# Weaving the attention of one token block into output projection and MLP of the block before

## The chip, the cores and the metric

The kernel runs on one NeuronCore of one Trainium2 chip. The metric is device microseconds (us) from the start to the end of one execution; the median of several executions is compared. The core has five engines that run at the same time and meet only at semaphores: PE (TensorE, the matmuls), DVE (VectorE), ACT (ScalarE), POOL (GpSimd), and SP (SyncE), which issues the DMAs here. Each engine takes its instructions strictly in the order in which they were written for it: a wait holds up everything behind it.

## The reference

One layer over 2048 prompt tokens (16 tiles of 128) and 64 sample tokens (tile 17, against 512 cached keys). All matrices are float32; each big product is computed as three fast products of a high part and a rest (hi·hi, hi·lo, lo·hi).

```python
gla_in, (sq, sk, sv), gate = project(xp, *lw)       # RMSNorm, x @ w_in (1024 x 3088)
S_p, o_g = gla_prompt(*gla_in)                      # gated linear attention, 4 heads
o_s = sb_prompt(sq, sk, sv)                         # stick-breaking attention, 8 heads of 64
xp = finish(xp, o_g, gate, o_s, *tail)

def sb_block(q, q_pos, k, v, k_pos):                # causal, 128 queries at a time
    z = einsum(q, k) * SB_HD ** -0.5
    log_beta = log_sigmoid(z)
    l = where(mask, log_sigmoid(-z), 0.0)
    c = cumsum(l, axis=3, reverse=True) - l         # from the last key to the first
    w = where(mask, exp(log_beta + c), 0.0)
    return einsum(w, v)

def finish(x, o_gla, gate, o_sb, gla_norm_g, w_out, norm2_g, w_up, w_down):
    mix = concatenate([og, o_sb])
    h = x + mix @ w_out                             # 1024 x 1024
    u = rmsnorm(h, norm2_g) @ w_up                  # 1024 x 4096
    return h + square(relu(u)) @ w_down             # 4096 x 1024
```

The causal mask makes attention grow with the position: tile t of the prompt has t + 1 tiles of 128 keys, the sample tile has 5.

## The kernel before

Five phases run one after the other, each with its own semaphores and an all-engine barrier at its end: `phase_project`, `phase_gla`, `phase_attention` (line 1043), `phase_output`, `phase_mlp`. They hand data on through DRAM.

`phase_attention` goes over heads outside and over 25 units inside; a unit is one query tile with up to 8 (or, cut in two, up to 8 at a time of 16) key tiles. There are 200 units with 1128 tiles of 128 x 128 scores, 141 for each head. A unit passes through these steps: PE makes the logits `z` (lines 1156 and 1157, and 1159 for the mask); ACT takes |z| (1213), exp (1224) and ln (1229); DVE makes the negated softplus (1251), sets the scan's start value (1257 or 1261) and runs the reverse scan over the keys (1267), and for a cut unit saves the sum (1272); ACT makes the weights (1219); PE transposes them tile by tile (1169); DVE copies them to SBUF (1281); PE multiplies them with the values (1185, in two instructions for each tile); DVE copies the result out (1290). `slot` on each engine fixes by hand which step of which unit comes next. `z` is double buffered, so that the logits of unit u + 1 wait for the scan of unit u - 1. The operands of a head are loaded one head ahead (`load_head`), those of head 0 during `phase_gla`.

`phase_output` has all 17 tiles in a pipeline: transpose `mix` (1396), split it, 48 matmuls of 512 columns with `w_out`, which was split during attention by POOL (1406), add x (1462), norm (1440, 1478, 1480, 1464), transpose (1414), split, store h and its transposed halves to DRAM.

`phase_mlp` has 4 token blocks (4, 4, 4 and 5 tiles, the last with 576 columns in two cuts of 288). For each block it goes over 16 generations of 256 hidden columns: `up` (1616), relu and square, `down` (1630), and DVE adds each result into `ya` (1752). Each generation's weights are loaded, ACT makes the high part, POOL the rest of `w_up` (1710) and DVE the rest of `w_down` (1733); the halves are double buffered. The matmuls of a generation read:

```python
for c in range(KC):
    for bank, at, size in cuts:
        mm = pe.matmul(pu[:, f, bank, 0:size], w[:, p, c, f * P:(f + 1) * P], xx[:, b % 2, c, at:at + size],
                       start=(i == 0 and c == 0), stop=(i == 2 and c == KC - 1))
```

Of the kernel before, what the change touches and what calls it, by code (L numbers as in the profile page):

```python
# [7 lines left out]

# [11 lines left out]
P = 128  # L20
# [626 lines left out]
def phase_gla(nc, gqk, gv, sgate, la, gla_g, state_in, ident, sum_mats, end_mat, score_mask, mix, new_state, pad_values, load_first):  # L647


    with Pool(nc, "gl") as m:  # L650
# [41 lines left out]
        s_am, s_vz, s_hin, s_hv = m.sem("am"), m.sem("vz"), m.sem("hin"), m.sem("hv")  # L692
# [23 lines left out]
        def _(sp):  # L716
# [15 lines left out]
            def slot(h, p, stages, sample):  # L732
# [11 lines left out]
                if 3 in stages:  # L744
                    h2, p2, t2 = before(h, p, 2)
                    sp.wait_ge(s_mo, t2 + 1)
                    sp.dma_start(mix[bass.ds(t2 * P, P), 0:512], mo[:, p2]).then_inc(s_md[p2], 16)
# [7 lines left out]
                if isinstance(h, int) and h * 2 + p == 1:  # L755
                    sp.wait_ge(s_vz, 1)
                    load_first(sp, s_hin, s_hv)

            pipeline(sp, slot)
            sp.wait_ge(s_hin, 80)  # L760
            sp.wait_ge(s_hv, 48)
# [116 lines left out]
        def _(dve):  # L878
            dve.memset(pad_values, 0.0).then_inc(s_vz, 1)
# [122 lines left out]
def attention_operands(m):  # L1002

    kt = m.sb("kt", [P, 2, KEYS], F32R)
    qh = m.sb("qh", [P, 2, ROWS], F32R)
    ql = m.sb("ql", [P, 2, ROWS], F32R)
    v = m.sb("v", [P, 2, KEYS // P, HD])
    return kt, qh, ql, v


def load_head(sp, operands, h, p, qT, kT, new_v, cache_v, s_in, s_v):

    kt, qh, ql, v = operands

    def head(ap):
        return ap[bass.ds(h, 1)].rearrange("o p k -> p (o k)")

    sp.dma_start(raw(kt[:, p]), head(kT)).then_inc(s_in, 16)
    for half in range(2):
        ps = slice(64 * half, 64 * half + 64)  # L1020
        sp.dma_start(raw(qh[ps, p]), head(qT)[0:64]).then_inc(s_in, 16)
        sp.dma_start(raw(ql[ps, p]), head(qT)[64:128]).then_inc(s_in, 16)
    cols = bass.ds(h * HD, HD)
    sp.dma_start(v[:, p, 0:SEQ // P], new_v[0:SEQ, cols].rearrange("(t p) c -> p t c", p=P)).then_inc(s_v, 16)
    sp.dma_start(v[:, p, SEQ // P:NEW_KEY_COL // P], cache_v[:, cols].rearrange("(t p) c -> p t c", p=P)).then_inc(s_v, 16)
    sp.dma_start(v[0:DEC, p, NEW_KEY_COL // P], new_v[SEQ:SEQ + DEC, cols]).then_inc(s_v, 16)
# [16 lines left out]
def phase_attention(nc, operands, qT, kT, new_v, cache_v, ident, diag_mask, mix, w_out, wh, wl):  # L1043
# [13 lines left out]
    with Pool(nc, "sb") as m:  # L1057
# [186 lines left out]
        def _(dve):  # L1244
# [58 lines left out]

            turns(dve, slot)

# [534 lines left out]
```

## Time and profile before

| | us |
|---|---|
| median of 3 runs | 3550.8 |
| lowest, highest | 3543.4, 3557.4 |
| profiled execution, span | 3553.5 |
| of it projection and GLA (to 1012) | 1012 |
| attention (1012 to 1804) | 792 |
| output projection (1804 to 2066) | 262 |
| MLP (2066 to the end) | 1487 |

The profile is that of one execution; its page shows nothing around the span, and its span lies 2.7 us above the median and inside the range of the runs. Busy times are sums of durations of instructions. For PE they overlap and their ends are modelled, so PE's true pace is read from counts of matmuls in a stretch in which it never waits, not from the mean duration. A wait is put down to the engine that released it last.

### The profile page before, as it was taken

What the parts mean: (1) busy time and instruction counts of PE and PEld (TensorE: products, weight loads), DVE (VectorE), ACT (ScalarE), POOL (GpSimd) and SP (SyncE); (2) the same over time, 40 slices, a digit from 0 to 9 for tenths busy, and PEclk for the clock granted to TensorE, in tenths of its full rate; (3) what the DMA queues carried; (4) which work ended last, traced back from release to release, by engine and by line L of the source; (5) the groups of instructions that cost most, each with busy time, mean ns of one, the idle gap of its engine ahead of it and who ended that gap; (6) DMA issues with size and microseconds to landing.
All of it is one profiled execution on the core that took longest, in us unless ns stands there. A gap on an engine that the chain in (4) does not pass through costs nothing. (4 is left out here: it accounts for less than half of the span.)

```text
span 3553.5 us, 48415 instructions
## 1 busy us (share of the span) xinstructions
PE 3228.6 (91%) x17416; PEld 2740.7 (77%) x17416; DVE 2017.8 (57%) x2853; ACT 1362.9 (38%) x1711; POOL 581.0 (16%) x379
## 2 busy tenths in 40 slices
PE   6999999979977787877779969999999999999999
PEld 5878777867767676777768758888888888899898
DVE  3545453459979899999933334444444444444444
ACT  3332423112248787788822222222222222222221
POOL 2131313013340000000000022222222222211210
PEclk8999999978869899899989989999999999999999
DMA  4535353342242211122035673335323523242221
GB/s 156 185 132 184 119 177 115 107 128 80 80 114 55 56 37 44 32 55 55 7 108 189 189 258 101 96 95 190 102 97 95 195 94 94 95 143 76 83 83 39
DMA packets 283612, 385.83 MB, mean 109 GB/s; under 512 B 50049, under 2 KB 195730, under 8 KB 280402
## 3 DMA queue, kind: packets, MB, share of 16 engines
q1 hardware_dynamic: 283474, 384.03, 34.6%
q8 instruction: 81, 1.33, 0.2%
q14 instruction: 57, 0.47, 0.0%
HBM read 295.26 MB, written 88.74 MB: 108 GB/s over the span
## 5 line engine op out<-in xcount | busy, mean ns | idle before, releaser
L1710 POOL TENSOR_TENSOR ml_ul<-ml_ur,ml_uh 128x2048 fp32r<-128x2048 f32 x63 | 293.4, 4657 | 1136.0 <-ACT ml_uh L1658 1136.0
L1752 DVE TENSOR_TENSOR ml_ya<-ml_ya,ml_pd 128x1024 f32<-128x1024 f32 x272 | 331.6, 1220 | 259.2 <-PE ml_pd L1630 259.2
L1740 DVE TENSOR_TENSOR ml_r<-ml_r 128x512 f32<-128x512 f32 (+1 forms) x128 | 84.9, 705 | 495.6 <-ACT ml_th L1688 495.6
L1267 DVE TENSOR_TENSOR_SCAN sb_g<-sb_z,sb_g,sb_a 128x639 f32<-128x639 f32 (+7 forms) x200 | 342.4, 1712 | 4.9
L1630 PE MATMUL ml_pd<-ml_dh,ml_th 128*128 128x512 f32 x1088 | 336.4, 390 | 1.6 <-DVE ml_ya L1752 1.6
L1630 PE MATMUL ml_pd<-ml_dl,ml_th 128*128 128x512 f32 x1088 | 335.5, 390 | 0.0
L1630 PE MATMUL ml_pd<-ml_dh,ml_tl 128*128 128x512 f32 x1088 | 335.1, 389 | 0.0
L1156 PE MATMUL sb_z<-hd_kt,hd_qh 128*128 128x512 f32 (+3 forms) x360 | 157.0, 436 | 163.1 <-DVE sb_g L1267 87.4
L1665 ACT ACTIVATE ml_dh<-ml_dr 128x2048 fp32r<-128x2048 f32 x64 | 122.8, 1919 | 473.8 <-PE ml_pd L1630 469.8
L1185 PE MATMUL sb_po<-hd_v,sb_wt 128*128 128x64 f32 x2256 | 303.8, 287 | 0.0
L1185 PEld LDWEIGHTS sb_po<-hd_v,sb_wt 128*128 128x128 f32 x2256 | 293.4, 206 | 3.5
L1682 ACT ACTIVATE ml_r<-ml_pu 128x512 f32<-128x512 f32 (+1 forms) x128 | 78.2, 611 | 536.4 <-PE ml_pu L1616 536.4
L1616 PE MATMUL ml_pu<-ml_xh,ml_uh 128*128 128x512 f32 (+1 forms) x1280 | 264.8, 353 | 21.0 <-DMA ml_xh<-h_t_hi 20.4
L1616 PE MATMUL ml_pu<-ml_xl,ml_uh 128*128 128x512 f32 (+1 forms) x1280 | 264.9, 353 | 1.6 <-DMA ml_xl<-h_t_lo 1.6
L1616 PE MATMUL ml_pu<-ml_xh,ml_ul 128*128 128x512 f32 (+1 forms) x1280 | 263.3, 352 | 0.0
L1616 PEld LDWEIGHTS ml_pu<-ml_xh,ml_uh 128*128 128x128 f32 x1280 | 215.8, 189 | 53.2 <-DMA ml_xh<-h_t_hi 20.8
L1616 PEld LDWEIGHTS ml_pu<-ml_xl,ml_uh 128*128 128x128 f32 x1280 | 215.2, 189 | 32.5 <-DMA ml_xl<-h_t_lo 2.4
L1616 PEld LDWEIGHTS ml_pu<-ml_xh,ml_ul 128*128 128x128 f32 x1280 | 214.5, 188 | 30.1
L1630 PEld LDWEIGHTS ml_pd<-ml_dh,ml_tl 128*128 128x128 f32 x1088 | 204.3, 188 | 43.0
L1630 PEld LDWEIGHTS ml_pd<-ml_dl,ml_th 128*128 128x128 f32 x1088 | 204.2, 188 | 42.8
L1630 PEld LDWEIGHTS ml_pd<-ml_dh,ml_th 128*128 128x128 f32 x1088 | 201.9, 188 | 45.5 <-DVE ml_ya L1752 5.8
L1156 PEld LDWEIGHTS sb_z<-hd_kt,hd_qh 128*128 128x128 f32 x360 | 75.0, 208 | 209.6 <-DVE sb_g L1267 110.7
(168 smaller groups left out, 5702.6 us busy)
## 6 DMA issues: line engine op xcount, KB each, us to landing
ml_ur<-in_w_up SPq DMA_DIRECT2D x64, 1024.0 KB
ml_dr<-in_w_down SPq DMA_DIRECT2D x64, 1024.0 KB, 4.9
pj_wr<-in_w_in SPq DMA_DIRECT2D x48, 1024.0 KB, 5.5
k_t<-pj_stT SPq DMA_DIRECT2D x21, 512.0 KB, 3.2
hd_kt<-k_t SPq DMA_DIRECT2D x8, 1344.0 KB, 9.3
pj_xb<-in_x SPq DMA_DIRECT2D x17, 512.0 KB, 6.6
q_t<-pj_stT SPq DMA_DIRECT2D x17, 512.0 KB, 3.2
hd_qh<-q_t SPq DMA_DIRECT2D x16, 544.0 KB, 12.3
```

Of the source, the lines that this page charges most:

```text
L1156: pe.matmul(dst, qh[:, p, t * P:(t + 1) * P], keys, start=True, stop=False)
L1185: mm = pe.matmul(po[:, tt % 2, 0:HD], wt[:, place(gi, 4, NGR), c * P:(c + 1) * P], v[:, p, key], start=(first and j == 0 and c == 0), stop ...
L1267: ins = dve.tensor_tensor_scan(g[:, u % 2, n - 2::-1], z[:, u % 2, n - 1:0:-1], a[:, place(u, 3), n - 2::-1], g[:, u % 2, n - 1:n], ALU.ad ...
L1616: mm = pe.matmul(pu[:, f, bank, 0:size], w[:, p, c, f * P:(f + 1) * P], xx[:, b % 2, c, at:at + size], start=(i == 0 and c == 0), stop=(i ...
L1630: mm = pe.matmul(pd[:, q, n * 512:(n + 1) * 512], tt[:, p, f, j * P:(j + 1) * P], w[:, p, f, n * 512:(n + 1) * 512], start=(i == 0 and f = ...
L1665: act.activation(dh[:, p], dr[:], ACT.Copy).then_inc(s_dh, 1)
L1682: act.activation(dst, src, ACT.Relu).then_inc(s_r, 1)
L1710: pool.tensor_tensor(ul[:, p], ur[:], raw(uh[:, p]), ALU.subtract).then_inc(s_ul, 1)
L1740: dve.tensor_tensor(r[:, f, 0:n], r[:, f, 0:n], r[:, f, 0:n], ALU.mult).then_inc(s_sq, 1)
L1752: dve.tensor_tensor(ya[:, j], ya[:, j], pd[:, q], ALU.add).then_inc(s_ya, 1)
```

## The change

`phase_attention`, `phase_output` and `phase_mlp` become one `phase_stream`. The loop over heads moves inside a loop over the four token blocks. The attention of block 0 runs alone; that of block b + 1 is spread evenly over the output projection and MLP of block b; under block 3 there is none. Where each engine does what is worked out when the program is built: `dense_order` gives the order of PE's dense work, `Plan` gives each piece a time from fixed costs of a matmul, and `weave` puts the three parts of each attention slot at even distances into it, on each engine in the same way. Nothing of this phase is in a hardware loop.

```diff
+def dense_order():
+    for j in range(BT):
+        yield "mix", 0, 0, j
+    for b in range(NB):
+        nt = NTS[b]
+        for g in range(OG):
+            for j in range(nt):
+                yield "out", b, g, j
+                if g == OG - 1 and j >= 2:
+                    yield "hid", b, 0, j - 2
+        for j in range(nt - 2, nt):
+            yield "hid", b, 0, j
+        yield "up", b, 0, 0
+        for g in range(NFG):
+            if g + 1 < NFG:
+                yield "up", b, g + 1, 0
+            for j in range(nt):
+                yield "down", b, g, j
+            if b + 1 < NB and g >= NFG - 2:
...
+                    yield "mix", b + 1, 0, j
+def weave(plan, ranges, streams, parts):
+    for b in range(NB):
+        lo, hi = plan.region[b]
+        first, n = ranges[b]
+        slots = n + 5
+        for i in range(slots):
+            s = i - 1
+            def unit(k):
+                return first + s - k if 0 <= s - k < n else None
+            for k, part in enumerate(parts):
+                part(unit)
+                streams.to(lo + (hi - lo) * (i + (k + 1) / len(parts)) / slots - 1.0)
+    streams.to(plan.total + 1e9)
```

What PE's slot holds, for unit s of the block (`u(k)` is unit s - k):

```diff
+            def part0(u):
+                if u(2) is not None:
+                    transposes(u(2))
+
+            def part1(u):
+                if u(-1) is not None:
+                    logits(u(-1))
+
+            def part2(u):
+                if u(3) is not None:
+                    values(u(3))
```

ACT's three parts are exp and ln of unit s, the weights of unit s - 1, and |z| of unit s + 1. DVE's are the copy of the transposed weights of unit s - 2, the softplus and start value of unit s, and the scan of unit s with the copy of the result of unit s - 3. SP loads the next job's operands where a job's first unit comes by. The dense work of each engine lies between the parts.

A unit now has at most 4 key tiles (`UT = 4`, 512 columns), which makes 336 units: 32, 64, 96 and 144 in the four blocks, with 80, 208, 336 and 504 score tiles. Keys, queries and values are loaded for each head and block (40 instead of 21 key tiles for each head), one job ahead. `a` has two buffers instead of three, `tp` one bank instead of two:

```diff
-        a = m.sb("a", [P, 3, 1024])
+        a = m.sb("a", [P, 2, 512])
-        wt = m.sb("wt", [P, 4, 512])
+        wt = m.sb("wt", [P, 3, 512])
-        z = m.ps("z", [P, 2, 1024])
-        tp = m.ps("tp", [P, 2, 512])
+        z = m.ps("z", [P, 2, 512])
+        tp = m.ps("tp", [P, 512])
+        dp = m.ps("dp", [P, BANKS, 512])
```

All dense results go through the four banks of `dp` in turn. A bank is free again when ACT (relu) or DVE (all else) has read it:

```diff
+            def free(k):
+                if k >= BANKS:
+                    if plan.by_act[k - BANKS] - (plan.by_act[k - BANKS - 1] if k > BANKS else 0):
+                        pe.wait_ge(s_fa, plan.by_act[k - BANKS])
+                    else:
+                        pe.wait_ge(s_fd, plan.by_dve[k - BANKS])
```

The output projection works in 256 columns, in four generations of `w_out` for each block, which take turns in the buffers of `w_up` and `w_down` and are loaded and split anew for each block (72 generations of each buffer instead of 64). The weight halves are single buffered, and POOL makes the rests of both:

```diff
+                        mm = pe.matmul(dp[:, k % BANKS, 0:FG], xx[:, c, j * P:(j + 1) * P], ww[:, c, :],
+                                       start=(q == 0 and c == 0), stop=(q == 2 and c == KC - 1))
...
+            def up_splits():
+                for i in range(NB * GENS):
+                    yield gen_start(plan.u_end, i)
+                    act.wait_ge(s_ur, 16 * (i + 1))
+                    if i:
+                        act.wait_ge(s_full, plan.u_end[i - 1])
+                        act.wait_ge(s_ul, 2 * i)
+                    for k in range(2):
+                        c = slice(4 * k, 4 * k + 4)
+                        act.activation(uh[:, c], ur[:, c], ACT.Copy).then_inc(s_uh, 1)
...
+            def down_rests():
...
+                        pool.tensor_tensor(dl[:, k], dr[:, k], raw(dh[:, k]), ALU.subtract).then_inc(s_dl, 1)
```

h is built and kept in `ya` in SBUF: x is loaded there, the projection is added, then each MLP result; its norm and transposed halves go straight into `xh` and `xl`. DVE adds `down` results in pieces of 512 columns (544 instead of 272 of 1024). The attention result goes to SBUF (`ms`), only the GLA half of `mix` through DRAM. `phase_gla` no longer loads head 0.

## Rows read from the trace of the kernel before

**Rows 1.** The page's head.
```profile
span 3553.5 us, 48415 instructions
```

**Rows 2.** Busy by stage: us, busy (instructions) of PE, PEld, DVE, ACT, POOL, PEclk, DMA.
```profile
1012.50:1804.20 791.70, 620.84 (x4240) 558.82 (x4240) 715.85 (x1160) 625.63 (x803) 26.99 (x16) 0.91 0.22 51
1804.20:2066.00 261.80, 226.82 (x1088) 185.51 (x1088) 82.00 (x70) 55.95 (x71) 12.68 (x35) 0.93 0.57 180
2066.00:3553.50 1487.50, 1473.47 (x7104) 1250.62 (x7104) 648.35 (x593) 384.88 (x384) 293.40 (x63) 0.99 0.34 113
```

**Rows 3.** Who waited for whom after 1015: us in total, times, longest.
```profile
PE sb_z L1156 <- DVE sb_g L1267: 87.4, 95, 1.7
PE ml_pu L1616 <- DMA ml_xh<-h_t_hi: 20.4, 1, 20.4
```

**Rows 4.** Stretches of the MLP: all engines; the last block's; its L1630 alone.
```profile
2500.00:3000.00 500.00, 499.03 (x2202) 413.06 (x2201) 221.88 (x207) 137.27 (x138) 104.39 (x24) 1.00 0.35 114
...
3150.00:3450.00 300.00, 300.00 (x1755) 270.54 (x1754) 127.24 (x117) 71.58 (x70) 57.66 (x12) 1.00 0.26 82
...
3150.00:3450.00 300.00, 161.16 (x699) 129.29 (x698) 1.00 0.26 82
```

**Rows 5.** PE in attention, in order of time: start, us, instruction.
```profile
1386.38 0.50 PE L1156 MATMUL sb_z<-hd_kt,hd_qh 128*128 128x512 f32 x1 [1.50 <-DVE sb_ssum L1272]
...
1387.47 1.72 PE L1185 MATMUL sb_po<-hd_v,sb_wt 128*128 128x64 f32 x14
...
1388.92 0.92 PEld L1169 LDWEIGHTS sb_tp<-sb_idt,sb_w 128*128 128x128 f32 x8
```

**Rows 6.** Start of attention, and what its first four units take: start, us, instruction.
```profile
1015.42 0.34 SPq L1106 DMA_DIRECT2D sb_idt<-in_ident  x1
...
1020.74 0.48 DVE L1267 TENSOR_TENSOR_SCAN sb_g<-sb_z,sb_g,sb_a 128x127 f32<-128x127 f32 x1
...
1030.83 1.55 DVE L1267 TENSOR_TENSOR_SCAN sb_g<-sb_z,sb_g,sb_a 128x639 f32<-128x639 f32 x1
```

**Rows 7.** DVE in attention by shape: busy us, mean ns, idle before.
```profile
L1281 DVE COPY sb_wt<-sb_tp 128x512 f32<-128x512 f32 x208 | 141.1, 679 | 20.2 <-PE sb_tp L1169 19.9
...
L1267 DVE TENSOR_TENSOR_SCAN sb_g<-sb_z,sb_g,sb_a 128x511 f32<-128x511 f32 x16 | 20.4, 1275 | 1.0
...
L1251 DVE SCALAR_TENSOR_TENSOR sb_a<-sb_z,sb_a 128x512 f32<-128x512 f32 x16 | 10.9, 682 | 0.4
...
L1261 DVE TENSOR_TENSOR sb_g<-sb_ssum,sb_a 128x1 f32<-128x1 f32 x64 | 10.2, 159 | 6.2 <-issue 0.4
```

**Rows 8.** One ACT step of a unit of 512 columns.
```profile
1215.09 0.63 ACT L1224 ACTIVATE sb_a<-sb_a 128x512 f32<-128x512 f32 x1
```

**Rows 9.** The last tile's way through the output projection's norm.
```profile
2043.65 1.21 DVE L1462 TENSOR_TENSOR ot_hb<-ot_pp,ot_xb 128x1024 f32<-128x1024 f32 x1
...
2048.44 1.97 PE L1414 MATMUL ot_tb<-ot_idt,ot_hn 128*128 128x128 f32 x8 [7.02 <-DVE ot_hn L1464]
...
2051.50 1.22 DVE L1456 TENSOR_TENSOR ot_sl<-ot_tb,ot_sh 128x1024 fp32r<-128x1024 f32 x1 [3.12 <-ACT ot_sh L1434]
```

**Rows 10.** Lines of the MLP: ns least/median/most, first and last start.
```profile
L1710 POOL TENSOR_TENSOR ml_ul<-ml_ur,ml_uh x63: 4609/4615/4826, 2081.2 to 3471.6; 128x2048 fp32r<-128x2048 f32 x63
...
L1740 DVE TENSOR_TENSOR ml_r<-ml_r x128: 676/691/759, 2088.6 to 3522.9; 128x512 f32<-128x512 f32 x96, 128x576 f32<-128x576 f32 x32
```

**Rows 11.** A DMA of a head's operands: KB, us from issue to landing.
```profile
hd_ql<-q_t SPq DMA_DIRECT2D x16, 544.0 KB, 14.3
```

**Rows 12.** Attention with short units and with long ones; one instruction of the first.
```profile
1200.00:1250.00 50.00, 40.52 (x245) 37.54 (x244) 38.91 (x69) 32.43 (x50) 0.00 (x0) 0.76 0.45 99
1650.00:1700.00 50.00, 38.69 (x287) 34.92 (x287) 49.28 (x75) 41.98 (x49) 0.00 (x0) 0.98 0.00 1
...
1223.24 0.22 DVE L1290 COPY sb_os<-sb_po 128x64 f32<-128x64 f32 x1 [3.46 <-issue]
```

**Rows 13.** DVE's last instruction of the kernel.
```profile
3548.25 1.22 DVE L1752 TENSOR_TENSOR ml_ya<-ml_ya,ml_pd 128x1024 f32<-128x1024 f32 x1 [1.50 <-PE ml_pd L1630]
```

More of the change, by code:

```diff
@@ new lines, with attention_jobs @@
+NTS = [BT] * FULL_BLOCKS + [LAST_BT]
+TOKENS = [BT * P] * FULL_BLOCKS + [BT * P + DEC]
+W = LAST_BT * P
+FG = 256
+FC = FG // P
+NFG = D_FF // FG
+OG = D // FG
+GENS = OG // 2 + NFG
+BANKS = 4
+UT = 4
+NK = BT * FULL_BLOCKS + BT
+Job = namedtuple("Job", "block heads keys sample")
+Unit = namedtuple("Unit", "job e h tile n lo first last")
+def attention_jobs():
+    jobs = []
+    for b in range(NB):
+        jobs += [Job(b, (h,), BT * (b + 1), False) for h in range(SB_HEADS)]
+    jobs += [Job(NB - 1, (h, h + 1), PAST // P + 1, True) for h in range(0, SB_HEADS, 2)]
+    return jobs
@@ new lines, in attention_units @@
+def attention_units(jobs):
+    units = []
+    for k, job in enumerate(jobs):
+        for e, h in enumerate(job.heads):
+            for i in range(1 if job.sample else BT):
+                n = job.keys if job.sample else BT * job.block + i + 1
+                hi = n
+                while hi > 0:
+                    lo = (hi - 1) // UT * UT
+                    units.append(Unit(k, e, h, BT if job.sample else i, hi - lo, lo, hi == n, lo == 0))
+                    hi = lo
+    return units
@@ L1091, in turns @@
-        def turns(eng, slot):
-            def unit(s, last):
-                return lambda k: s - k if 0 <= s - k and not (last and s - k >= NU) else None
-            for s in range(LEAD):
-                slot(0, s, unit(s, False))
-            with eng.Fori(0, SB_HEADS // 2 - 1) as i:
-                for s in range(LEAD, NU + LEAD):
-                    slot(i, s, unit(s, False))
-            for s in range(LEAD, NU + LEAD):
-                slot(SB_HEADS // 2 - 1, s, unit(s, True))
+        gb = m.sb("gb", [P, D])
@@ new lines, in transposes, with values @@
+            def transposes(u):
+                pe.wait_ge(s_w, u + 1)
+                if u >= 1:
+                    pe.wait_ge(s_wt, u)
+                for c in range(units[u].n):
+                    mm = pe.transpose(tp[:, c * P:(c + 1) * P], w[:, u % 2, c * P:(c + 1) * P], idt[:])
+                mm.then_inc(s_tr, 1)
+            def values(u):
+                un = units[u]
+                p = un.job % 2
+                tt = tiles_done[u]
+                if u == job_first[un.job]:
+                    pe.wait_ge(s_v[p], v_need[un.job])
+                if un.first and tt >= 1:
+                    pe.wait_ge(s_of, tt)
+                pe.wait_ge(s_wt, u + 1)
+                for c in range(un.n):
+                    mm = pe.matmul(po[:, tt % 2 * HD:(tt % 2 + 1) * HD], wt[:, u % 3, c * P:(c + 1) * P],
+                                   v[:, p, un.e * jobs[un.job].keys + un.lo + c],
+                                   start=(un.first and c == 0), stop=(un.last and c == un.n - 1))
+                mm.then_inc(s_pv, 1)
```

1163 lines of the change are left out of this document (542 added, 621 removed).

## The prediction

> **What bounds the kernel now.** I read the table by stage first, then each stage for the wait that ends last. Attention and what follows take 3553.5 - 1012.5 = 2541 us of the span [rows 1, 2]; the 1012 us before are untouched. Two different engines bound this part. In the MLP PE is busy 1473 of 1487 us at clock 0.99, and in 500 us of it PE issues 2202 matmuls of 512 columns, one in 0.227 us [rows 2, 4]: that is PE's pace, and nothing of it can be hidden. The output projection is bound by PE too (227 of 262 us). In attention DVE is busy 716 of 792 us while PE's busy time is 621 us at clock 0.91 [rows 2], and PE's largest wait there is that of the logits for DVE's scan [rows 3]. So for 792 us PE waits on DVE, and for 1487 us DVE is busy only 648. The change lays the two over each other. The question is what PE's work adds up to, and how much of it the in-order queues let through.
>
> **PE's sum after the change.** Paces first, at full clock. 512 columns: 0.227 us. 288 columns: in the last block's stretch 699 of 1755 matmuls are of 512 columns and take 159 us; the other 1056 share 141 us, 0.134 each [rows 4]. The trace has no run of split products of 256 columns; on the line through the two paces they take 0.121. The bounds are 0.114 (half of a 512) and 0.134 (a 288); I take the line. A score tile of attention costs: logits 1.09 us for 8 tiles, 0.136; values 14 instructions in 1.72 us, less some 0.2 for the last one's drain, two for each tile, 0.22 to 0.23; transpose 8 in 0.92, 0.115 [rows 5]. With the mask that is 0.50.
>
> - MLP: 5568 matmuls of 512 and 1536 of 288 columns: 1264 + 206 = 1470 us. Unchanged; the trace's own stage agrees once its start is taken off.
> - Output projection: 17 tiles x 4 x 24 = 1632 matmuls of 256 columns, 198 us (before 816 of 512, 185 us): +13 us (bounds +1 to +34).
> - Its 272 transposes: 272 x 0.129 (the slower of the paces of a transpose, since fewer stand together) = 35 us.
> - Attention of blocks 1 to 3: 1048 tiles x 0.50 = 524 us. The 80 tiles of block 0 are in the lead-in.
>
> Lead-in. Attention starts at 1015.4 and its first scan is at 1020.7, on operands loaded during GLA [rows 6]. Now the constants and five loads of job 0 are issued first (about 0.4 us for each issue), and land some 4 to 8 us later (14.3 us was for a head of 544 KB beside others [rows 11]; the pieces are now 128 to 256 KB): first scan at about 1027, +6 us (bounds +2 to +14). Then 32 units of 1 to 4 tiles: the first four of before go from scan to the scan of the fifth in 10.1 us, of which the fifth's longer softplus is 0.4: 2.4 us a unit [rows 6], 77 us. The last unit needs three more slots, then the first tiles are transposed and split: dense work begins at about 1111.
>
> Removed and put at nothing more: the barriers and DMA waits between phases, 20.4 us at the MLP's start [rows 3] and PE's idle time in the projection's stage (262 us, 227 busy [rows 2]), the round trips of h through DRAM and the loop turns. They are gaps in the table of stages and aren't in the new sum.
>
> Floor: 1111 + 1470 + 198 + 35 + 524 = 3338.
>
> Added on PE's path. **The norm** stands four times between the last projection tile and `up`. The last tile of before shows the chain: add at 2043.65, square, POOL, scale, transposes at 2048.44, rest done at 2052.7, 9.1 us with PE idle for 7.0 before its transposes [rows 9]. It is now in smaller pieces, but POOL may be in a half split of 4.6 / 2 = 2.3 us [rows 10] when the norm's step reaches it: 8 us each, 32 us. In blocks 0 to 2 attention matmuls lie nearby, but PE's queue is in order and they don't move past the waiting transposes. **Tail:** DVE's last add to the end of the store, 5 us as before [rows 1, 13]. That gives 3375, the least that the new order allows. **Turn of the block:** y must leave `ya` before x comes in, two transfers of 512 KB behind each other, under 10.9 us of projection work for each column group: mostly hidden, 5 us in all (bounds 0 to 30).
>
> **What the queues cost.** Attention 1 to 3 is spread over about 390 us of dense PE time each. With attention's own matmuls a slot of PE is (390 + 104) / 69 = 7.2 us, (390 + 168) / 101 = 5.5 us and (390 + 252) / 149 = 4.3 us. Now DVE, for a full unit: copy 0.68, softplus 0.68, start value 0.16, scan 1.28, sum 0.16 (as the start value) [rows 7], with the steps between them about 3.05 us. Block 3's 144 units (112 full) need 342 + 61 = 403 us of DVE; the dense work beside them 16 x (4 steps on the hidden columns of 0.69 [rows 10] and 8 adds of 512 columns, a little over half of the 1.22 of 1024 columns [rows 9], 0.65) = 127, and 23 for projection and norm. That is 553 of 641 us, 86%. Smaller units are no gain here: 200 units become 336, and 64 pairs of `ssum` steps become 200, +43 us of DVE; moved off DVE are the 64 splits of `w_down`. ACT has about 2.6 us for a full unit (four steps of 0.63 [rows 8]), 470 us in this stretch, 73%. POOL has 288 halves of 2.3 us, 665 us in all, hidden in 2440.
>
> But shares don't decide; the round trip does. Logits of unit u + 1 wait for the scan of unit u - 1, so two slots can't be shorter than: logits 0.7, |z| 0.6, exp and ln 1.26, softplus and start 0.95, scan and sum 1.5, six hand-overs of about 0.1: 5.6 us [rows 5, 7, 8], plus what dense work stands in ACT's and DVE's queues between these steps, on average another 2 to 2.7 us (a split half of 1024 columns, 1.0; a relu, 0.6; an add, 0.65). About 8.0 us against two slots of 14.4, 11.0 and 8.6. In block 1 this never ends last, in block 2 where splits meet (15 us), in block 3 often: four split halves in each of some 14 generations, each of which can put 1.0 us into the trip, are 56 us. Beside `down` DVE has 3.05 + 1.9 adds of 0.65 = 4.3 us a slot and its waits for the step in front, against PE's 4 x 0.50 + 2.6 = 4.6; I put 0.3 us on each of some 80 such slots, 24 us. Together 80 + 15 + 5 = 100 us. This is the weakest term: bounds 0 (all slack is enough) and 300 (below). I take 100 since the trip lies just under the slot in one block of three.
>
> **Sum:** 3375 + 5 + 100 = 3480 for this execution; the median of the runs is 2.7 us below its span, so 3477, 2.1% below 3550.8. Its own range is 3430 to 3530.
>
> **The rivals.**
> - **PE alone sets the time.** The queues' slack suffices and PE never waits in blocks 1 to 3: 3375 to 3430, say 3380. For it: PE's waits for the scan in attention were 0.9 us on average and 1.7 at most [rows 3], and there are 3 us of slack in a slot of block 1. Against it: 86% of DVE in block 3.
> - **The round trip sets the time (slower).** If dense work in ACT's and DVE's queues makes the trip 12 us for two slots rather than 8, block 3 takes 149 x 6.0 = 894 us instead of 641, and block 2 606 instead of 558: 3380 + 253 + 48 = 3681. The place is the wait of `logits` for the scan. It decides from a trip of about 10.8 us (5.4 us a slot): 149 x (5.4 - 4.3) = 164 us eats the whole gain. For it: `z`, `tp` and `a` lost buffers and every piece of dense work sits inside the trip. Against it: 2.4 us a unit was reached for short units [rows 6].
> - **The clock.** Beside short units the granted clock was 0.76, with PE as busy (40.5 of 50 us) as in a stretch at 0.98 (38.7 us); in the first, all engines stood still for some 3 us at the loop's turn [rows 12]. The levels are 1.2 and 2.4 GHz, so 0.91 over attention [rows 2] is full clock with stretches at half. If the woven 1676 us ran at 0.91, they cost 166 us more: 3380 + 166 = 3546, no change. Against it: the MLP's dense matmuls at 0.99 to 1.00 [rows 4] are between the attention's now. By the Trainium skill (TensorE: Matmul & The Clock Gate, "Why this matters for your kernels") an idle PE goes to the low clock and sustained matmuls bring it back; by that rule, only the four norms and the lead-in would run slow.
> - **POOL and DVE block each other.** The rests of `w_down` move to POOL, which is then busy for 27% of the phase. If a step of DVE on the hidden columns (both inputs in SBUF, 256 of them) had to wait for a running POOL half, that is 256 x 0.27 x 1.15 = 80 us of DVE, of which the 64 in block 3's stretch count, 20 us, and some in block 2's: 3505. Against it: such steps took 676 to 759 ns with POOL busy beside them [rows 10], so nothing waits within its duration. The Trainium skill (SBUF — State Buffer, "Who interferes with whom") states it as a lock that makes the second instruction wait in full; it speaks against moving work to POOL.
> - **Loads come late.** If a job's operands took the 14.3 us of [rows 11] in the lead-in, 8 jobs last 14.3 instead of 9.6 us: +38, 3520.
>
> **Chances.** Forecast 0.42; PE alone 0.20; round trip 0.18; clock 0.09; POOL 0.05; loads 0.06. A difference under 0.5% (18 us) can't be told from none in this kernel. Faster by more (below 3533): the forecast, PE alone, POOL and most of the loads, 0.72. Within: the clock's case and bits of its neighbours, 0.09. Slower: the round trip and a bit, 0.19. The range that should hold the time 8 times in 10 is 3380 to 3640: it leaves out half of "PE alone" and about half of "round trip".
>
> **What will show it.** The first scan near 1027 and the first projection matmul near 1111 (right within 15 us). Stretches in block 1's part with PE without waits and at clock 1.0. In block 3's part (about 1900 to 2600) waits of PE's logits for the scan of 50 to 100 us in all; over 200 is the round trip, under 20 is PE alone. Four gaps of about 7 us before the norm's transposes. The last block at the old pace, 480 to 490 us. DVE's durations for the hidden steps above 0.8 us, or its waits beside POOL, would show the lock. Wrong altogether it would be if PE's pace for 256 columns, or for attention's short matmuls between dense ones, is not what [rows 4, 5] give: each 10 ns on the 1632 matmuls and on attention's some 4400 instructions in blocks 1 to 3 are 16 and 44 us.

## The result, and the profile after

| | before | changed |
|---|---|---|
| median, us | 3554.1 (4 runs) | 3710.4 (4 runs) |
| lowest, highest | 3543.4, 3560.3 | 3701.3, 3711.5 |
| profiled execution, span | 3553.5 [rows 1] | 3699.6 |
| attention, projection and MLP, from 1015 on | 2538 | 2685 |

The ratio is 1.0428, with a 95% interval of 1.0407 to 1.0449: the changed kernel is 4.3% slower. The forecast was 3477 and its range ended at 3640: it was 233 us too low and wrong in sign. The woven order itself is not what costs: the experiments end with the same weave at 3456 us, after one change to what DVE reads, one to which buffer a weight generation uses and one to a small place of the order.

Busy time by stage of the changed kernel. The columns are those of [rows 2], with the DMA's GB/s behind. The stages are the dense work of blocks 0, 1, 2 and 3 (the lead-in before them took 102 us), the first three with the attention of the next block in them, the last with none.

```profile
1117.00:1692.00 575.00, 528.51 (x2779) 443.58 (x2777) 346.09 (x555) 254.21 (x424) 178.18 (x79) 0.96 0.30 90
1692.00:2343.00 651.00, 593.12 (x3223) 502.00 (x3224) 442.11 (x714) 330.99 (x551) 182.24 (x81) 0.96 0.29 89
2343.00:3126.00 783.00, 683.82 (x3818) 578.91 (x3817) 558.94 (x938) 428.68 (x727) 185.26 (x82) 0.94 0.27 82
3126.00:3695.00 569.00, 516.49 (x3019) 464.17 (x3018) 206.72 (x261) 123.17 (x186) 173.72 (x78) 0.94 0.20 65
```

No engine is busy all the time: PE is at 87 to 92% in the four dense stages and DVE never above 71%. By the forecast's paces blocks 0 to 2 need 411 us of PE each without attention (1536 matmuls of 512 columns, 384 of 256, 64 transposes, 8 us for the norm), with 208, 336 and 504 tiles at 0.50 then 515, 579 and 663, and block 3 needs 499. They took 60, 72, 120 and 70 more. The last block is the telling one: it has no attention at all, yet it lost as much as the first two. So the loss can't be only attention's round trip. Who PE waited for from 1015 on, the lead-in included (us in all, times, longest):

```profile
PE st_z L1366 <- DVE st_g L1649: 68.3, 43, 5.2
PE st_dp L1487 <- DVE st_ya L1730: 43.9, 24, 2.3
PE st_z L1366 <- DVE st_ssum L1654: 42.0, 22, 4.8
PE st_dp L1466 <- POOL st_ul L1758: 25.6, 4, 6.4
...
PE st_tp L1377 <- DVE st_wt L1662: 20.2, 13, 3.2
...
PE st_dp L1414 <- DMA st_mg<-mix: 12.8, 3, 12.4
PE st_dp L1487 <- DVE st_xl L1684: 12.7, 3, 4.2
...
PE st_dp L1487 <- issue: 6.0, 1, 6.0
```

DVE is behind most of these, in the logits (L1366), in `down` (L1487) and in the transposes (L1377), though it is idle for 29% of the third stage and for more of the others. A wait of 5.2 us for one scan is four scans long. So I looked at how long DVE's own instructions lasted (ns least/median/most, first and last start; then the groups by shape: busy us, mean ns, idle before):

```profile
L1718 DVE TENSOR_TENSOR st_tl<-st_r,st_th x128: 691/760/2811, 1197.1 to 3662.0; 128x512 fp32r<-128x512 f32 x96, 128x576 fp32r<-128x576 f32 x32
L1642 DVE TENSOR_TENSOR st_g<-st_ssum,st_a x200: 159/159/2376, 1130.4 to 3071.9; 128x1 f32<-128x1 f32 x100
...
L1718 DVE TENSOR_TENSOR st_tl<-st_r,st_th 128x512 fp32r<-128x512 f32 x96 | 165.4, 1723 | 3.3
L1642 DVE TENSOR_TENSOR st_g<-st_ssum,st_a 128x1 f32<-128x1 f32 x200 | 81.9, 409 | 18.2
L1716 DVE TENSOR_TENSOR st_r<-st_r 128x512 f32<-128x512 f32 x96 | 76.2, 794 | 261.2 <-ACT st_th L1606 261.2
```

L1718 (hidden rest, `tl = r - th`) takes 1.72 us on average. In the kernel before, the same step (L1743) took 677 to 753 ns. L1642 (start value of the scan, one element in each partition) takes 0.41 us against 0.159 [rows 7], and 2.38 at most. One L1718 in two is held up: 63 of the 128 took 2.71 to 2.81 us, the others at most 0.76. Over all instructions that is about 131 us more on L1718 (128 x 1.02), 50 on L1642 and 11 on L1716 (the square): 192 us of DVE. All three take both operands from SBUF. L1649, the scan, reads `a` from SBUF and `z` from PSUM and keeps its 1277 ns.

One place of the last block, in order of time (start, us, instruction; in brackets the idle time before it and what ended it):

```profile
3416.23 5.25 POOL L1758 TENSOR_TENSOR st_ul<-st_ur,st_uh 128x1024 fp32r<-128x1024 f32 x2 [8.05 <-ACT st_uh L1555]
...
3418.45 0.81 DVE L1716 TENSOR_TENSOR st_r<-st_r 128x576 f32<-128x576 f32 x1 [6.92 <-ACT st_th L1606]
...
3419.29 2.81 DVE L1718 TENSOR_TENSOR st_tl<-st_r,st_th 128x576 fp32r<-128x576 f32 x1
...
3422.02 2.47 DVE L1730 TENSOR_TENSOR st_ya<-st_ya,st_dp 128x512 f32<-128x512 f32 x4
...
3422.75 1.10 PE L1487 MATMUL st_dp<-st_dh,st_th 128*128 128x512 f32 x2 [2.28 <-DVE st_ya L1730]
...
3423.65 1.05 PE L1487 MATMUL st_dp<-st_dl,st_th 128*128 128x512 f32 x2
```

POOL's two halves run from 3416.23 to 3421.48. L1718 is released at 3419.29, inside the second half, and ends at 3422.10, 0.62 us behind POOL: it did its work when POOL had finished. Behind it DVE's queue holds the adds that free the banks of `dp`, so PE waits 2.28 us. It then goes on at half pace: 0.425 us a matmul instead of 0.227 until about 3426.2, 8 matmuls in 3.46 us where full clock needs 1.82. So this collision costs PE 2.3 us of waiting and 1.6 of slow clock. In attention the same happens to the smallest instruction of all:

```profile
2811.27 4.75 POOL L1765 TENSOR_TENSOR st_dl<-st_dr,st_dh 128x1024 fp32r<-128x1024 f32 x2 [19.41 <-ACT st_dh L1565]
2811.31 2.38 DVE L1642 TENSOR_TENSOR st_g<-st_ssum,st_a 128x1 f32<-128x1 f32 x1
...
2815.12 0.50 PE L1366 MATMUL st_z<-st_kt,st_qh 128*128 128x512 f32 x1 [0.42 <-DVE st_g L1649]
```

It comes 0.04 us behind POOL's start and ends as POOL's first half does (2.37 us, half of the 4.75). These rows fit the rule in the Trainium skill (SBUF — State Buffer, "Who interferes with whom"): a DVE instruction with two SBUF inputs and a GpSimd instruction that reads SBUF use one read port, and the second is blocked in full. That such a lock costs the time is theory A. Theory B is that the in-order queues and the round trip cost it, and that the long durations lie in DVE's slack.

### The profile page after: what moved, and what is told of

The parts are those of the page before. It is cut to its first block and busy times, and to the rows that moved or that the text cites. A ratio compares the mean times of both kernels' runs of the same rounds, so it can differ in the third digit from the quotient of the medians.

```text
span 3699.6 us, 49868 instructions
## 1 busy us (share of the span) xinstructions
PE 3302.8 (89%) x18184; PEld 2798.4 (76%) x18184; DVE 2193.4 (59%) x3664; ACT 1498.3 (40%) x2479; POOL 975.7 (26%) x588
## 5 line engine op out<-in xcount | busy, mean ns | idle before, releaser
L1758 POOL TENSOR_TENSOR st_ul<-st_ur,st_uh 128x1024 fp32r<-128x1024 f32 x144 | 370.1, 2591 | 961.9 <-ACT st_uh L1555 961.9
L1765 POOL TENSOR_TENSOR st_dl<-st_dr,st_dh 128x1024 fp32r<-128x1024 f32 x144 | 342.8, 2402 | 939.5 <-ACT st_dh L1565 939.5
L1730 DVE TENSOR_TENSOR st_ya<-st_ya,st_dp 128x512 f32<-128x512 f32 x544 | 365.5, 682 | 167.1 <-PE st_dp L1487 164.8
L1487 PE MATMUL st_dp<-st_dh,st_th 128*128 128x512 f32 x1088 | 381.4, 423 | 62.5 <-DVE st_ya L1730 43.9
L1716 DVE TENSOR_TENSOR st_r<-st_r 128x512 f32<-128x512 f32 (+1 forms) x128 | 101.2, 790 | 486.7 <-ACT st_th L1606 486.7
L1649 DVE TENSOR_TENSOR_SCAN st_g<-st_z,st_g,st_a 128x127 f32<-128x127 f32 (+3 forms) x336 | 371.5, 1106 | 19.7 <-DVE st_g L1642 0.5
L1487 PE MATMUL st_dp<-st_dh,st_tl 128*128 128x512 f32 x1088 | 377.4, 420 | 0.0
L1487 PE MATMUL st_dp<-st_dl,st_th 128*128 128x512 f32 x1088 | 372.7, 419 | 0.0
L1390 PEld LDWEIGHTS st_po<-st_v,st_wt 128*128 128x128 f32 x2256 | 322.2, 204 | 28.8 <-DVE st_ms L1672 2.0
L1466 PE MATMUL st_dp<-st_xh,st_uh 128*128 128x512 f32 (+1 forms) x1280 | 307.8, 373 | 30.7 <-POOL st_ul L1758 25.6
L1390 PE MATMUL st_po<-st_v,st_wt 128*128 128x64 f32 x2256 | 310.6, 280 | 2.1 <-DVE st_ms L1672 1.6
L1487 PEld LDWEIGHTS st_dp<-st_dh,st_th 128*128 128x128 f32 x1088 | 212.2, 201 | 114.0 <-DVE st_ya L1730 54.0
L1366 PE MATMUL st_z<-st_kt,st_qh 128*128 128x128 f32 (+3 forms) x336 | 137.7, 410 | 131.5 <-DVE st_g L1649 68.3
L1487 PEld LDWEIGHTS st_dp<-st_dl,st_th 128*128 128x128 f32 x1088 | 213.4, 200 | 42.3
L1487 PEld LDWEIGHTS st_dp<-st_dh,st_tl 128*128 128x128 f32 x1088 | 213.3, 201 | 42.0
```

The lines of the kernel that those rows point to most:

```text
L1366: pe.matmul(dst, qh[:, p, q0:q0 + P], keys, start=True, stop=False)
L1390: mm = pe.matmul(po[:, tt % 2 * HD:(tt % 2 + 1) * HD], wt[:, u % 3, c * P:(c + 1) * P], v[:, p, un.e * jobs[un.job].keys + un.lo + c], sta ...
L1466: mm = pe.matmul(dp[:, k % BANKS, 0:size], ww[:, c, f * P:(f + 1) * P], xx[:, c, at:at + size], start=(q == 0 and c == 0), stop=(q == 2 an ...
L1487: mm = pe.matmul(dp[:, k % BANKS, :], tt[:, p, f, j * P:(j + 1) * P], ww[:, f, n * 512:(n + 1) * 512], start=(q == 0 and f == 0), stop=(q ...
L1649: ins = dve.tensor_tensor_scan(g[:, u % 2, n - 2::-1], z[:, u % 2, n - 1:0:-1], a[:, u % 2, n - 2::-1], g[:, u % 2, n - 1:n], ALU.add, ALU ...
L1730: dve.tensor_tensor(part, part, dp[:, k % BANKS], ALU.add).then_inc(s_fd, 1)
```

## The experiments

**POOL only writes.** The rests become constants, so part of the weight products is left out; POOL's steps keep their length and their place.

```diff
-pool.tensor_tensor(ul[:, c], ur[:, c], raw(uh[:, c]), ALU.subtract).then_inc(s_ul, 1)
+pool.wait_ge(s_ul, 2 * i + k)
+pool.memset(raw(ul[:]), 0.0).then_inc(s_wo, 1)
+pool.wait_ge(s_wo, wo())
+pool.memset(raw(ul[:, 4 * k:4 * k + 2]), 0.0).then_inc(s_ul, 1)
```

> The changed kernel, with POOL's rests of the weights replaced by memsets of about the same length (128x2048, then 128x512 elements, for each half). They write the rests as zero, so the low parts of the weights are left out of the result; POOL reads no SBUF. Everything else, the order and the waits included, is as in the changed kernel. Theory A (POOL's reading subtractions block DVE's steps with two SBUF inputs: in the changed kernel the step on line 1718 took 1722 ns on average and that on line 1642 409 ns, where 700 and 159 are its cost alone): both fall to their cost alone, some 190 us of DVE time go, and with PE's slow stretches behind them the kernel comes down from 3700 to between 3460 and 3540. Theory B (the round trip from logits to the scan through the queues sets the time): the trip keeps its steps, so the time stays at 3660 or more.

3517.3 us (one run). Its DVE, grouped by shape, has no long instruction left, while POOL is as busy as before (1.81 us and a second memset of 0.53 for each half):

```profile
L1719 DVE TENSOR_TENSOR st_tl<-st_r,st_th 128x512 fp32r<-128x512 f32 x96 | 66.5, 692 | 3.3
L1643 DVE TENSOR_TENSOR st_g<-st_ssum,st_a 128x1 f32<-128x1 f32 x200 | 31.9, 160 | 18.2
...
L1766 POOL MEMSET st_ul<- 128x2048 f32 x144 | 260.7, 1811 | 951.7 <-ACT st_uh L1556 943.2
```

63 of the 128 L1719 lie beside a memset, as 63 of L1718 lay beside a rest, and keep their time. So it is POOL's reading that matters, not its length or the order of the queues: some 190 us.

**DVE reads one SBUF input.** Everything is computed. The square is made in place in the PSUM bank, the rest is taken from there, and the start value gets its subtrahend as a scalar operand.

```diff
-dve.tensor_tensor(top, ssum[:], a[:, u % 2, n - 1:n], ALU.subtract)
+dve.tensor_scalar(top, a[:, u % 2, n - 1:n], ssum[:], -1.0, ALU.subtract, ALU.mult)
...
-dve.tensor_tensor(r[:, f, 0:n], r[:, f, 0:n], r[:, f, 0:n], ALU.mult).then_inc(s_rr, 1)
+    dve.tensor_tensor(dp[:, k % BANKS, 0:size], dp[:, k % BANKS, 0:size], r[:, f, at:at + size], ALU.mult).then_inc(s_rr, 1)
...
+    ins = dve.tensor_tensor(tl[:, gg % 2, f, at:at + size], dp[:, k % BANKS, 0:size], raw(th[:, gg % 2, f, at:at + size]), ALU.subtract)
```

> The changed kernel with full arithmetic and POOL's work untouched; only DVE's steps get one SBUF input. The square of the hidden values is made in the PSUM bank (bank times the relu in SBUF), the rest is bank minus high part, so each of the two reads PSUM and SBUF; the banks of up are then freed by DVE. The start value of the scan is made by a tensor_scalar with the sum as its scalar operand. Theory A: the long steps on DVE vanish (700 ns or less for 512 columns, 160 for the start value), POOL's halves fall back to 2.31 us, time 3470 to 3560, against a median of 3710 for the change. If a scalar operand counts as a second SBUF input, line 1642's step stays at 400 ns and about 50 us of the gain in blocks 0 to 2 are missing. Theory B: 3680 or more, since the trip is as long as before.

3518.3 us (3514.8 to 3521.0), ratio to before 0.9897 [0.9875, 0.992]. Here POOL's rests are as they were, and DVE's steps are short:

```profile
L1720 DVE TENSOR_TENSOR st_tl<-st_dp,st_th 128x512 fp32r<-128x512 f32 x96 | 66.5, 692 | 10.0
L1639 DVE TENSOR_SCALAR st_g<-st_a,st_ssum 128x1 f32<-128x1 f32 x200 | 42.8, 214 | 18.8
...
L1763 POOL TENSOR_TENSOR st_ul<-st_ur,st_uh 128x1024 fp32r<-128x1024 f32 x144 | 341.5, 2392 | 956.4 <-ACT st_uh L1552 956.4
```

Taking the lock away from either side gives the same time, and in this experiment nothing is left out of the result. PE's waits now:

```profile
PE st_z L1366 <- DVE st_g L1646: 27.1, 28, 2.7
PE st_dp L1463 <- POOL st_ul L1763: 23.7, 4, 5.9
...
PE st_dp L1484 <- DVE st_tl L1720: 17.2, 14, 1.2
PE st_dp L1443 <- DVE st_r L1702: 16.2, 4, 5.4
PE st_dp L1411 <- DMA st_mg<-mix: 13.1, 3, 12.1
...
PE st_z L1366 <- DVE st_ssum L1651: 10.6, 11, 2.3
PE st_dp L1443 <- DVE st_hn L1702: 8.0, 4, 5.7
```

The logits' waits for the scan and the sum fell from 110 to 38 us: two thirds of what looks like theory B in the changed kernel was the lock, handed on. The waits at the second `w_down` generation are those of the changed kernel, 12.7 and 6.0 us.

**Which of the two steps.** First the start value alone is mended, then the hidden steps alone.

> The changed kernel with one line of e3: the start value of the scan (128 x 1) by a tensor-scalar operation, whose subtrahend goes in as the scalar operand, not as a second SBUF tensor; the squares and hidden rests still read two SBUF inputs. All arithmetic is there. It splits the 192 us between changed kernel (3710) and e3 (3518). Sum by DVE's excess in the changed kernel's trace: 50 us at the start values, 142 at squares and rests. Theory P (each is paid in proportion, all of it reaches PE): 3655 to 3665. Theory Z (PE's waits for the running sums, 110 us in the changed kernel against 38 in e3, are all the start values'): 3630 to 3645. Theory H (the start values wait beside other work and cost nothing; it is the hidden rests): 3695 to 3710.

> e3 with one line put back: the start value of the scan reads two SBUF tensors again (128 x 1), the squares and hidden rests keep their PSUM input. All arithmetic is there. Theory P: 3518 + 50 = 3570. Theory Z: 3585 to 3595. Theory H: 3518 to 3530. If e9 and e10 together give less than the 192 us or more than it, the two locks cover each other or feed each other.

3700.3 us (two runs), ratio 1.0397 [1.034, 1.0454], and 3541.4 us, ratio 0.9953 [0.9931, 0.9975]. By the ratios, times 3554: the start values cost 11 us beside locked hidden steps (1.0428 - 1.0397; the intervals overlap, so this may be nothing) and 20 us without them (0.9953 - 0.9897). The hidden steps cost 169 to 178 us (1.0428 - 0.9953, 1.0397 - 0.9897). DVE's own excess was 50 and 142 us. Theory P (in proportion) fails. The first kernel lies in the range of H, the second between H (up to 3530) and P (3570): nearly all of it is the hidden steps. They cost more than their own excess. In the timelines shown, a late hidden rest stands ahead of the adds that PE needs, and in one of them the clock fell behind it; a late start value stands in a trip that has slack in most slots. That this is the reason is argued, no run separates it. Theory Z took the logits' waits for the start values' own; with those mended alone they are still 62.6 + 41.5 us, with the hidden steps mended alone 41.2 + 13.4.

**The dense work alone.** Attention of blocks 1 to 3 and of the sample tile is left out, once in the changed kernel, once in the one with one SBUF input.

```diff
-        jobs += [Job(b, (h,), BT * (b + 1), False) for h in range(SB_HEADS)]
-    jobs += [Job(NB - 1, (h, h + 1), PAST // P + 1, True) for h in range(0, SB_HEADS, 2)]
+        if b == 0:
+            jobs += [Job(b, (h,), BT * (b + 1), False) for h in range(SB_HEADS)]
```

> The changed kernel with the attention of blocks 1 to 3 and of the sample tile left out (the projection gets stale attention results there); block 0's attention, and the dense work of all four blocks, are in place, in the same order. PE's work after 1117 us is then 1693 us at full clock. Theory A: the blocks lose about 4 us in each of 64 generations also without attention, as the last block does in the changed kernel: 3050 to 3110. Theory B: without round trips only the norm's four waits and the four waits of about 6 us for the second generation of w_up remain: 2880 to 2920.

> As e3 (no step of DVE reads two SBUF inputs in the blocks), but the attention of blocks 1 to 3 and of the sample is left out, as in e5 (3156 us), so the two differ only in the lock. Theory A (the lock between POOL's rests and DVE's steps costs the dense part alone some 2.7 us of each of the 64 MLP generations): the period of two generations' worth of work falls from 24.6 us to about 21.9, 3156 - 173 = 2983, and the wait for the squares and hidden splits (128 us in e5) nearly goes. Theory T (without attention the generation is too short for the chain up, ACT, DVE, down whatever DVE's speed): 3080 to 3150, the wait stays over 60 us.

3156.0 and 2994.0 us (one run each): 162 us for 64 generations, 2.5 for each, with nothing of attention in their queues. In the first, PE waits 128.3 us in 59 waits for `ya`, none of which is left in the second (17.2 us in 14 waits for `tl` are). The long steps are not attention's doing: in the first of these two kernels, the hidden rests take what they take in the changed kernel, and one generation looks like another:

```profile
L1719 DVE TENSOR_TENSOR st_tl<-st_r,st_th 128x512 fp32r<-128x512 f32 x96 | 164.8, 1717 | 3.3
```

```profile
2000.98 2.01 ACT L1555 ACTIVATE st_uh<-st_ur 128x1024 fp32r<-128x1024 f32 x2 [4.39 <-PE st_dp L1466]
...
2002.12 5.18 POOL L1759 TENSOR_TENSOR st_ul<-st_ur,st_uh 128x1024 fp32r<-128x1024 f32 x2 [6.45 <-ACT st_uh L1555]
...
2005.11 2.74 DVE L1719 TENSOR_TENSOR st_tl<-st_r,st_th 128x512 fp32r<-128x512 f32 x1
...
2008.50 0.72 PE L1487 MATMUL st_dp<-st_dh,st_th 128*128 128x512 f32 x2 [2.14 <-DVE st_ya L1731]
```

ACT splits the weights until 2002.99 and then makes `th` (L1606 at 2003.51); POOL starts on the one, DVE on the other, and they meet, once in each generation. In the changed kernel it is the same: the square starts 2.05 to 2.22 us behind POOL's first half in 63 of the 64 generations, the hidden rest behind it is held. PE goes on at full pace behind the wait of 2.14 us here, so the clock doesn't fall behind each of these waits. Theory A holds for the difference, 162 us against 173. The first kernel is still slower than I had put it, 3156 against 3050 to 3110. That isn't the lock: without it the same work takes 2994, where theory B's range was 2880 to 2920. Of the 74 us above it, 48 are waits of PE that the range left out (17.2 for `tl`, 18.7 at the second `w_down` generation, 12.6 for the DMA of the mix); the rest is open.

**Before, with the rests of w_down on POOL.** Can the lock be had in the kernel before by its largest part of the change alone?

```diff
+            def split_down(b, g, p):
+                pool.wait_ge(s_dh, number(b, g) + 1)
+                pool.tensor_tensor(dl[:, p], dr[:], raw(dh[:, p]), ALU.subtract).then_inc(s_dl, 1)
...
-            def split_down(b, g, p):
-                dve.wait_ge(s_dh, number(b, g) + 1)
-                dve.tensor_tensor(dl[:, p], dr[:], raw(dh[:, p]), ALU.subtract).then_inc(s_dl, 1)
```

> The kernel before, with one part of the change alone: the rests of w_down are made by POOL (64 more subtractions of 128x2048) and no longer by DVE. Phases, buffers and double buffering of the weights are those of before; DVE has 156 us less to do in a stage in which it was busy 648 of 1487 us. Theory A: POOL is now reading while DVE squares and splits the hidden values; those steps wait for up to 4.6 us, the adds queue behind them, and the MLP becomes 100 to 200 us longer: 3650 to 3750. Theory B has no mechanism here, since there is no attention in the MLP: 3530 to 3560.

3579.1 us (one run), 28 above the median of before in that series (3551.1, up to 3563.2): neither theory. The hidden rests stay short, and so do the squares but for four of 128 (ns least/median/most). Those four squares, and no others, began while POOL was at work, and took 2.66 to 4.71 us:

```profile
L1744 DVE TENSOR_TENSOR ml_r<-ml_r x128: 676/692/4714, 2099.2 to 3546.7; 128x512 f32<-128x512 f32 x96, 128x576 f32<-128x576 f32 x32
```

The longest, behind a rest of `w_down` (start, us, instruction):

```profile
2484.44 4.61 POOL L1714 TENSOR_TENSOR ml_dl<-ml_dr,ml_dh 128x2048 fp32r<-128x2048 f32 x1
...
2484.88 4.71 DVE L1744 TENSOR_TENSOR ml_r<-ml_r 128x512 f32<-128x512 f32 x1 [10.72 <-ACT ml_th L1688]
```

POOL is busy twice as long as before, and hardly ever at the same time as those steps. The timeline of the kernel before shows why (start, us, instruction); this is its generation, the same every 21.8 us:

```profile
2514.88 1.29 DVE L1740 TENSOR_TENSOR ml_r<-ml_r 128x512 f32<-128x512 f32 x2 [7.78 <-ACT ml_th L1688]
2515.26 1.91 ACT L1658 ACTIVATE ml_uh<-ml_ur 128x2048 fp32r<-128x2048 f32 x1
2516.09 1.28 DVE L1743 TENSOR_TENSOR ml_tl<-ml_r,ml_th 128x512 fp32r<-128x512 f32 x2
2517.25 4.62 POOL L1710 TENSOR_TENSOR ml_ul<-ml_ur,ml_uh 128x2048 fp32r<-128x2048 f32 x1 [17.14 <-ACT ml_uh L1658]
2517.29 1.21 DVE L1752 TENSOR_TENSOR ml_ya<-ml_ya,ml_pd 128x1024 f32<-128x1024 f32 x1
```

There ACT makes `th` first and splits the whole of `w_up` after it. POOL starts at 2517.25, 0.12 us before DVE's last two-input step ends (2516.09 + 1.28 = 2517.37), so here DVE is the first of the two, and what DVE does beside POOL from then on is L1752, with one input in PSUM. Of this experiment's 28 us, 7 are waits of PE for `ya` (8.6 against 1.6 before) behind the long squares; where the others went is open.

**POOL hardly works.** POOL computes 16 of 256 or 64 of 1024 columns of each rest; the other columns are left out.

> As the changed kernel, but POOL computes only 16 of 256 or 64 of 1024 columns of each part of the weight rests (the others stay zero), so that POOL hardly reads SBUF and its latency is gone too; e1 wrote constants of the same length instead (3517 us). Part of the weight rests is left out. Theory A (all that POOL costs is the lock, and its own length at the two refills in one buffer): e1 less the 24 us of waits for the rests of the second w_up generation, 3490 to 3500. Theory U (POOL's 4.7 us per generation sets the pace in the blocks beyond that): under 3470. Theory B (POOL does not matter): as e1, 3515 to 3520.

3481.0 us (one run), 36 below the kernel in which POOL only writes. PE's 4 waits for `ul` are 10.2 us against 24.6 there, and its waits at the second `w_down` generation 7.4 against 19.5. The time lies between theories A and U (24 and over 50 us), and 26.5 of the 36 us are waits at these places: POOL's length counts mainly where one buffer is used twice in a row.

**Weight generations take strict turns.** This starts from the kernel with one SBUF input. There up1 follows up0, and down15 follows down14, in one buffer; here each goes into the other one.

```diff
+SEQ_G = [("out", g) for g in range(OG)] + [("up", 0), ("up", 1)]
+for _g in range(NFG - 2):
+    SEQ_G += [("down", _g), ("up", _g + 2)]
+SEQ_G += [("down", NFG - 2), ("down", NFG - 1)]
```

> This kernel is the one with one-SBUF-input steps (e3, 3518 us), with the weight generations in strict turn between the two buffers: out0 to out3, up0, up1, down0, up2, down1, ... up15, down14, down15. In e3 up1 follows up0 in the same buffer, and down15 follows down14 in the same buffer, so that the second is split into its parts only when PE has done with the first. All arithmetic is there. Theory R (these refills stall PE): in e3 PE waits 23.7 us in 4 waits for the rests of the second w_up generation and 12.7 + 6.0 us in 3 waits at the second w_down generation in a row; both go, 42 us, and the slow clock behind them with them: 3470 to 3485. Theory S (the waits are slack of DVE or ACT that shows there and is paid elsewhere when they go): 3505 to 3520.

3462.0 us (3458.2 to 3475.5), ratio 0.975 [0.9719, 0.978], 52 us less by the ratios. The waits for `ul` are gone, and of the 18.7 us at the second `w_down` generation 4.8 are left. Theory R holds, with 8 us more than its range; the waits that went are 38 us.

**The mix transposes of the last block between tiles.** On top of the one before.

> As e6, and the second half of the mix transposes of the last block, which e3 and e6 issue in a row behind the last down projection of block 2, stands between the tiles of that down projection. All arithmetic is there. In e3 PE waits once 12.1 us for the DMA that stages the mixes there. Theory R: the DMA then runs beside the down tiles; 10 to 15 us below e6. Theory S: the transposes wait for the same attention steps wherever they stand, and the wait only moves: within 4 us of e6.

3456.1 us (3449.9 to 3462.4), ratio 0.9717 [0.9692, 0.9741]. The waits for this DMA fell from 12.9 to 4.5 us; the intervals of the two ratios overlap, so a gain of some 6 us is likely but not settled. This is the fastest version: 2.8% below the kernel before, and it computes everything.

## Why the prediction was wrong

**The step that failed: POOL and DVE block each other.** It was among the rivals, with 20 us and a chance of 0.05; it cost some 190 us by the two experiments that remove it, more than the 156 us that the change lost. Of the 233 us between forecast and result it is 192 (3710 less 3518); the other 41 are under "The sum, again". The sign named for it, hidden steps above 0.8 us, came. Three things were wrong in it.

- The argument against it. "Such steps took 676 to 759 ns with POOL busy beside them" was read from [rows 10], which give durations and the first and last start of each line. They don't say that the two ran at once. No L1740 did; L1743 met POOL's start in 55 of 128 cases, by 0.34 us at most, and DVE was first. POOL was busy in the same stage, not at the same time. And the trace of before does show the lock, on another line: five of the 64 rests of `w_down` (L1733, two SBUF inputs) began while POOL's L1710 ran and took 3.19 to 4.33 us, all others stayed at 2.29. The row shows it (ns least/median/most):

```profile
L1733 DVE TENSOR_TENSOR ml_dl<-ml_dr,ml_dh x64: 2291/2293/4332, 2083.6 to 3510.2; 128x2048 fp32r<-128x2048 f32 x64
```

- The price of a step. I took the chance of meeting POOL as its busy share, 0.27, at 1.15 us. That is 0.31 us a step; measured were 1.02 on L1718. The times aren't independent: ACT's order lets POOL's half and DVE's square start within 2.3 us of each other in nearly every generation, with attention beside them or without. And I counted the two hidden steps and no other; the 200 start values read two SBUF inputs as well.
- Where it lands. I let only 64 of the steps count, those in block 3's stretch, and some of block 2's, since DVE has slack elsewhere. But the step stands ahead of the adds that free PE's banks. PE then waits although DVE's share is 36% in the last block, and in the place shown its clock falls behind the wait. That block took 569 us, where I had named 480 to 490.

**PE's sum.** The first scan came at 1029.1 (forecast 1027), the first dense transpose at 1110.6 and the first projection matmul at 1117.0 (1111 for both): right. The paces of attention and of 256 columns were a little high. The fastest version, in two stretches in which PE doesn't wait (start, us, instruction):

```profile
2424.28 0.39 PE L1397 MATMUL st_z<-st_kt,st_qh 128*128 128x512 f32 x1
...
2424.73 0.39 PE L1519 MATMUL st_dp<-st_uh,st_tl 128*128 128x512 f32 x1
...
2425.65 1.00 PE L1421 MATMUL st_po<-st_v,st_wt 128*128 128x64 f32 x8
2426.46 0.48 PE L1519 MATMUL st_dp<-st_ul,st_th 128*128 128x512 f32 x1
2426.78 0.62 PE L1519 MATMUL st_dp<-st_uh,st_tl 128*128 128x512 f32 x2
...
2941.52 1.10 PE L1460 MATMUL st_dp<-st_uh,st_xh 128*128 128x256 f32 x8
2942.45 1.10 PE L1460 MATMUL st_dp<-st_ul,st_xh 128*128 128x256 f32 x8
```

Starts are what counts. Logits of 4 tiles 0.45 us, their values 0.81, and the dense matmul behind these 0.32 instead of 0.227; with the transposes (0.35, and 0.09 behind them, in the same stretch) 1.79 us a unit, 0.45 a tile instead of 0.50: 52 us less over 1048 tiles. 8 matmuls of 256 columns take 0.93 us (0.934 over a longer stretch), 0.117 each instead of 0.121, 7 us less.

**The norm.** 24.2 us in 8 waits of the kernel with one SBUF input (16.2 + 8.0), against 32: right in kind, a little high.

**The round trip.** 100 us, called the weakest term; with the lock gone the logits wait 38 us, 22 of them in block 3's part. Its mechanism is there, at the low side of its bounds of 0 to 300. In the changed kernel these waits are 52 us in block 3's part (2343 to 3126), inside the 50 to 100 that I had named as the sign of the forecast, while the kernel was 233 us slower than it: such a sign can't tell a late trip from a late engine within it. The durations, named in the same paragraph, could.

**What was missed.** The second generation in a row in one buffer: 25.6 us for `ul` and 18.7 at `down` (12.7 + 6.0), 52 us when mended. That the halves are single buffered was named in the change and never costed. Also the DMA of the last block's mix, 12.8 us.

**The clock.** The rival of 0.91 over the woven part didn't come: 0.94 to 0.96, and 0.97 to 0.98 with the lock gone. In the lead-in it was 0.69 in the changed kernel. At 3422.75 it fell and PE had just waited; short attention work between dense matmuls did not lower it, since the three woven blocks are at 0.97 to 0.98 as the last one is.

**The sum, again.** The kernel with one SBUF input stands at 3518, 38 above the forecast of 3480. The forecast's terms put right, from its waits and the paces above: -59 for the paces, -62 for the round trip, -8 for the norm, +24 and +19 for the generations in one buffer, +13 for the DMA, +17 for the waits for `tl`: 3424. Of the 94 us that are left, low clock can be up to 66: 0.98, 0.97, 0.97 and 0.97 over the four blocks of 542, 603, 717 and 533 us mean 133 us at the lower level, half of which is lost if PE works all through it. The rest is open. So the forecast is only 38 us from the kernel without the lock, and that is in part luck: 129 us of terms too high stand against 73 us of terms left out and 94 that no term explains.

## What to carry to other kernels

Before work is moved to POOL or to another time, list which of DVE's instructions read two tensors from SBUF (the smallest too), and look at the longest duration of each. If it is normal, look in the timeline for whether they ever ran beside a POOL instruction that reads SBUF. A duration that stayed normal proves something only where the two overlapped. If they will meet, give DVE one input from PSUM or as a scalar operand; a share of busy time is no chance of a meeting when both are released by the same engine. And a buffer cut from two to one costs where the order uses it twice in a row: walk through the order's ends for such places.

## What the runs showed of the hardware

- A DVE step of 128x1 with two SBUF inputs waits for a POOL instruction that reads SBUF as a large one does: 2.38 us instead of 0.159. The wait lies within the reported duration and no wait view names it.
- The tensor-scalar form of 128x1, both inputs in SBUF, one as the scalar operand, took 212 to 218 ns in all 200 instructions, 54 of which lie beside a rest on POOL. An input in PSUM frees a step too (692 ns on average at 512 columns). The price is 0.055 us for the scalar form.
- POOL memsets of about the same length (1.81 and 0.53 us) don't hold DVE up: 693 ns in the median of L1719, 759 at most.
- POOL is held up as well: its halves of `w_up` took 2591 ns on average in the changed kernel, 2392 with the lock gone.
- Whichever of the two starts first keeps its time: where DVE's L1743 was 0.34 us from its end when POOL started, DVE kept its 0.75 us and POOL took 4.82 instead of 4.62 (kernel before).
- A PE wait of 2.3 us in dense work was followed by 3.5 us at half pace in the changed kernel; one of 2.14 us in the dense work alone was not.
